# A two-block transformer forward on one core: weight splits placed directly behind the end of a unit, own-engine waits only where a result is used, and the feed-forward loops written out

## The chip, the core and the metric

The kernel runs on one core of a Trainium2 chip. That core has a matrix engine (PE, TensorE), a vector engine (DVE), a scalar engine (ACT), a general engine (POOL) and a sync engine (SP) that here issues only DMAs. Each engine runs its own instructions in order; they meet only at semaphores. The metric is the device time of one execution in microseconds, lower is better.

## The reference

The input is one sequence of 512 tokens with 1024 channels, f32. Block 1 has two layers, block 2 has two layers, and a norm ends each block. The parts with most of the arithmetic are dense products with weights:

```
# block 1, twice
h = h + 0.5 * swiglu_ffn(rms_norm(h, ffn1_norm), w_gate_up, w_down)     # 1024 -> 2*2816 -> 1024
q, k, v, ca, cg = split(rms_norm(h, mix_norm) @ w_in)                   # 14 chunks of 128
mixed = concat([rms_norm(window_attention(q, k, v)), rms_norm(conv31(ca * sigmoid(cg)))])
h = h + mixed @ w_out
h = h + 0.5 * swiglu_ffn(rms_norm(h, ffn2_norm), w_gate_up, w_down)
h = h + sigmoid(h @ w_ple_gate) * rms_norm(p @ w_ple, ple_norm)
# block 2, twice
h = h + concat([gated_deltanet, nsa, stick_breaking]) @ w_out
g, u = split(rms_norm(h) @ w_gate_up)                                   # each through a causal 3-tap conv
h = h + (silu(conv3(g)) * conv3(u)) @ w_down
h = h + sigmoid(rms_norm(h) @ w_ple_gate) * rms_norm(p @ w_ple, ple_norm)
```

## The kernel before

Activations are held transposed: 128 channels on the partitions, 512 tokens along the free axis, eight chunks for the 1024 channels and 22 for the 2816 of the feed-forward. Every dense product is exact to f32 level by splitting both factors into a high and a low half: with activations `xh`, `xl` and weights `wh`, `wl`, PE adds `xh*wh`, `xl*wh` and `xh*wl` (lines L400, L401, L402).

**Units.** The weights stream in 564 units of 128x1024 (512 KB each) through four `raw` buffers. ACT copies a unit to its high half (`act_split`, L380), DVE subtracts that for the low half (`dve_split`, L385), each with two buffers, and PE turns a unit into one 128x512 result in one of two PSUM banks `DB`. A unit of eight chunks has 24 matmuls. The semaphores are `w_hi` and `w_lo` (halves ready), `unit` (PE has finished a unit), `bank` (its result has been read). ACT's split of unit k+2 needs the end of unit k, since it overwrites that unit's `wh`; PE starts unit k+2 when `w_lo` says so and the bank of unit k has been read. The next DMA into a `raw` buffer starts behind the DVE split that reads it.

**Feed-forward.** `ffn_units` cuts the 22 chunks into groups of 8, 8 and 6. Of each group first its gate and up units (two for each chunk), then the eight units of the down-projection, which has as many chunks as the group has. In the first part PE, ACT and DVE each run a hardware loop over pairs of chunks (`Fori`, L509, L522, L543), four units a turn. DVE reads gate (`gbuf`) and up (`ubuf`), multiplies them to `fbuf`, ACT makes `fh`, DVE makes `fl`, and `ff_lo` counts finished chunks. In block 2 each of them first goes through three taps (`act_conv_pair`, `dve_conv_pair`). In the down part DVE adds each result to `h` (L551); in the last group the new `h` chunk is at once split for the next stage (`act_tile` L431 to `xh`, `dve_tile` L467 to `xl`) and squared for its norm (`act_square` L440). All of this, as the split of the weights, stands in one hand-written order for each engine.

**The other dense stages** are straight code: IN (14 units of w_in, whose results are rotated or gated while ACT and POOL run the first 31-tap convolutions), OUT (8 units), GATE (8 units). In each step of them before, the split of unit k+1 comes after all other work of step k-1, and behind nearly every operation of ACT and DVE stands a wait for the engine's own semaphore (as `dve.wait_ge(s["w_lo"], st.up("w_lo"))`). Where a norm's reciprocal is needed (`dve_rstd`, L488; `rstd_e` in OUT of block 1, L1326), DVE makes it ahead of the first result of the stage.

## Time and profile before

| | us |
|---|---|
| median of 3 runs | 4252.59 (4246.54 to 4254.69) |
| profiled execution | 4251.98 |
| its span | 4250.2 |
| PE busy (share of the span) | 3960.5 (93%) |
| DVE busy | 2396.6 (56%) |
| ACT busy | 1667.6 (39%) |
| POOL busy | 471.4 (11%) |
| weight DMAs | 564 of 512 KB, 3.5 median from issue to landing |

The profiled execution has 1.8 us outside its span. A stage lies where its lines are busy: block 1's layer 0 runs FFN1 from 23, IN from 391, OUT from 621, FFN2 from 669 and GATE from 1035; its layer 1 starts at 1092 and its IN at 1454. Block 2's layer 0 has OUT from 2690, its feed-forward groups from 2738, 2860 and 3000 and GATE from 3135; the last GATE is at 4178. In a table of windows a row gives, for each engine, the busy time and in brackets the count of instructions, then PE's granted clock as a share of 2.4 GHz.

### The profile page before, as it was taken

What the parts mean: (1) busy time and instruction counts of PE and PEld (TensorE: products, weight loads), DVE (VectorE), ACT (ScalarE), POOL (GpSimd) and SP (SyncE); (2) the same over time, 40 slices, a digit from 0 to 9 for tenths busy, and PEclk for the clock granted to TensorE, in tenths of its full rate; (3) what the DMA queues carried; (4) which work ended last, traced back from release to release, by engine and by line L of the source; (5) the groups of instructions that cost most, each with busy time, mean ns of one, the idle gap of its engine ahead of it and who ended that gap; (6) DMA issues with size and microseconds to landing.
All of it is one profiled execution on the core that took longest, in us unless ns stands there. A gap on an engine that the chain in (4) does not pass through costs nothing. (4 is left out here: it accounts for less than half of the span.)

```text
span 4250.2 us, 51550 instructions
## 1 busy us (share of the span) xinstructions
PE 3960.5 (93%) x17866; PEld 3110.4 (73%) x17866; DVE 2396.6 (56%) x3149; ACT 1667.6 (39%) x2268; POOL 471.4 (11%) x366
## 2 busy tenths in 40 slices
PE   8999979999999997999989999899989999899997
PEld 6887657888788765788766677677767667777775
DVE  5455765445544576545667634756566663475656
ACT  4224643223322464322434444443343444343333
POOL 1001710000000171000000022100010012110001
PEclk9999989999999998999999989999999989899998
DMA  4333103333333310333321100222223100022221
GB/s 146 95 99 94 55 16 95 99 98 103 89 94 99 94 55 20 97 98 96 105 92 54 35 1 6 70 89 89 91 85 99 50 25 1 11 80 89 89 89 69
DMA packets 86995, 314.55 MB, mean 74 GB/s; under 512 B 10016, under 2 KB 10400, under 8 KB 86176
## 3 DMA queue, kind: packets, MB, share of 16 engines
q1 hardware_dynamic: 83664, 302.43, 22.7%
q10 hardware_dynamic: 3152, 9.74, 0.7%
q8 instruction: 111, 1.82, 0.2%
q14 instruction: 68, 0.56, 0.0%
HBM read 307.94 MB, written 2.10 MB: 73 GB/s over the span
## 5 line engine op out<-in xcount | busy, mean ns | idle before, releaser
L400 PE MATMUL ps<-xh,wh 128*128 128x512 f32 x2336 | 924.2, 396 | 59.3 <-DVE wl L385 40.7
L380 ACT ACTIVATE wh<-raw 128x1024 fp32r<-128x1024 f32 x564 | 598.4, 1061 | 896.2 <-PE ps L402 681.8
L385 DVE TENSOR_TENSOR wl<-raw,wh 128x1024 fp32r<-128x1024 f32 x564 | 712.6, 1263 | 419.5 <-ACT wh L380 399.8
L401 PE MATMUL ps<-xl,wh 128*128 128x512 f32 x2336 | 913.9, 391 | 0.0
L402 PE MATMUL ps<-xh,wl 128*128 128x512 f32 x2336 | 913.5, 391 | 0.0
L400 PEld LDWEIGHTS ps<-xh,wh 128*128 128x128 f32 x2336 | 441.5, 189 | 173.2 <-DVE wl L385 54.0
L400 PE MATMUL ps<-fh,wh 128*128 128x512 f32 x1280 | 511.7, 400 | 49.1 <-DVE fl L1467 28.5
L402 PEld LDWEIGHTS ps<-xh,wl 128*128 128x128 f32 x2336 | 441.2, 189 | 93.1
L401 PEld LDWEIGHTS ps<-xl,wh 128*128 128x128 f32 x2336 | 441.4, 189 | 92.7 <-issue 2.7
L401 PE MATMUL ps<-fl,wh 128*128 128x512 f32 x1280 | 503.6, 393 | 0.0
L402 PE MATMUL ps<-fh,wl 128*128 128x512 f32 x1280 | 502.6, 393 | 0.0
L400 PEld LDWEIGHTS ps<-fh,wh 128*128 128x128 f32 x1280 | 243.1, 190 | 124.0 <-DVE wl L385 38.8
L446 POOL TENSOR_TENSOR rstd<-rstd,sq 128x512 f32<-128x512 f32 x77 | 101.9, 1323 | 1798.3 <-ACT sq L440 1797.5
L402 PEld LDWEIGHTS ps<-fh,wl 128*128 128x128 f32 x1280 | 243.4, 190 | 52.4
L401 PEld LDWEIGHTS ps<-fl,wh 128*128 128x128 f32 x1280 | 243.6, 190 | 49.3 <-issue 0.5
L551 DVE SCALAR_TENSOR_TENSOR h<-ps,h 128x512 f32<-128x512 f32 x144 | 99.6, 692 | 282.7 <-PE ps L402 281.8
L410 PE MATMUL ps<-xh,wh 128*128 128x512 f32 x448 | 198.9, 444 | 25.0 <-PEq L1358 10.0
L733 POOL TENSOR_TENSOR y<-y,tap_out 128x512 f32<-128x512 f32 x120 | 171.9, 1432 | 109.4 <-ACT tap_out L934 101.6
L605 ACT ACTIVATE sbuf<-gbuf 128x512 f32<-128x512 f32 x88 | 55.7, 632 | 326.6 <-DVE gbuf L616 326.6
L412 PE MATMUL ps<-xh,wl 128*128 128x512 f32 x448 | 179.7, 401 | 0.0
L411 PE MATMUL ps<-xl,wh 128*128 128x512 f32 x448 | 179.1, 400 | 0.0
L616 DVE TENSOR_TENSOR gbuf<-ps,rstd 128x512 f32<-128x512 f32 x88 | 60.9, 692 | 155.4 <-PE ps L402 154.6
(464 smaller groups left out, 5270.2 us busy)
## 6 DMA issues: line engine op xcount, KB each, us to landing
raw<-in_w SPq DMA_DIRECT2D x564, 512.0 KB, 3.5
con<-in_consts SPq DMA_DIRECT2D x1, 2052.5 KB, 14.3
h<-in_x SPq DMA_DIRECT2D x4, 512.0 KB, 7.6
p_t<-in_p ACTq DMA_DIRECT2D x4, 512.0 KB, 3.6
w1k<-in_w1c ACTq DMA_DIRECT2D x2, 1024.0 KB, 4.8
w1v<-in_w1c ACTq DMA_DIRECT2D x2, 1024.0 KB, 6.9
out<-h SPq DMA_DIRECT2D x8, 256.0 KB, 2.0
dup_k<-roped ACTq DMA_DIRECT2D x8, 128.0 KB, 2.4
```

The lines of the kernel that those rows point to most:

```text
L380: nc.scalar.activation(wh[k % 2][:, :], raw[k % 4][:, :], ACT.Copy).then_inc(s["w_hi"], 1)
L385: nc.vector.tensor_tensor(wl[k % 2][:, :], raw[k % 4][:, :], wh[k % 2][:, :].bitcast(F32), ALU.subtract).then_inc(s["w_lo"], 1)
L400: nc.tensor.matmul(DB[k % 2][:, :], a, hi(q), start=(q == order[0]), stop=False)
L401: nc.tensor.matmul(DB[k % 2][:, :], a, lo(q), start=False, stop=False)
L402: last = nc.tensor.matmul(DB[k % 2][:, :], b, hi(q), start=False, stop=(q == order[-1]))
L410: nc.tensor.matmul(DB[k % 2][:, :], a, hi(q), start=start and n == 0, stop=False)
L411: nc.tensor.matmul(DB[k % 2][:, :], a, lo(q), start=False, stop=False)
L412: last = nc.tensor.matmul(DB[k % 2][:, :], b, hi(q), start=False, stop=stop and n == len(chunks) - 1)
L446: nc.gpsimd.tensor_tensor(acc[:, :], acc[:, :], sq[:, n % 2, :], ALU.add).then_inc(s["sq_add"], 1)
L551: nc.vector.scalar_tensor_tensor(h[:, j, :], DB[k % 2][:, :], factor, h[:, j, :], ALU.mult, ALU.add).then_inc(s["bank"], 1)
L616: v.tensor_tensor(gbuf[:, :], DB[k % 2][:, :], rstd[:, :], ALU.mult).then_inc(s["bank"], 1)
L733: nc.gpsimd.tensor_tensor(y[:, ct, :], y[:, ct, :], tap_out[:, i % 3, :], ALU.add)\
```

## The change

It has five parts.

- In both splits, the tiles, the squares and the feed-forward bodies the wait for the engine's own semaphore is left out, except where the next operation reads what was just written.
- In the down part of a feed-forward and in IN, OUT and GATE, the split of unit k+2 stands directly behind the read (DVE) or the end (ACT) of unit k, ahead of tile, square, sigmoid, taps and the like. In the swiglu body ACT splits before the silu.
- The loops over pairs of chunks on PE, ACT and DVE are written out: there are six feed-forwards (two in each layer of block 1, one in each of block 2) of three groups, so 18 such stretches, and on each of the three engines none of them is a hardware loop now. PE's program grows from 10536 rows to 14407, DVE's from 2589 to 2947, ACT's from 1767 to 1886.
- `AHEAD = 3`: of the first down unit of a group PE runs all chunks but the last, then three chunks of the second unit, then the last chunk of the first, then the rest of the second.
- In block 2's body the low half `fl` of a chunk is made behind the first read of the next chunk, and ACT starts both first taps before the silu. In the last pair of a group the split of the second down unit comes at the end. In OUT the reciprocals for the embedding's norm move behind the first read.

The diff, cut to its core:

```diff
+AHEAD = 3
...
             nc.scalar.activation(wh[k % 2][:, :], raw[k % 4][:, :], ACT.Copy).then_inc(s["w_hi"], 1)
-            act.wait_ge(s["w_hi"], st.up("w_hi"))
...
                                     ALU.subtract).then_inc(s["w_lo"], 1)
-            dve.wait_ge(s["w_lo"], st.up("w_lo"))
...
-                with pe.Fori(start, n // 2) as i:
+                for i in range(start, n // 2):
                     for k in range(4):
                         pe_unit(pe, s, i, u + k, x_hi, x_lo)
-                for j in range(DC):
-                    k = u + 2 * n + j
-                    wait = (lambda q: ("ff_lo", ff_before + pair + q + 1)) if j == 0 else None
-                    pe_unit(pe, s, 0, k, f_hi, f_lo, n, wait)
-
-        def act_ffn(act, s, st, base, ff_before, gain, x_n, sq_n, pair_body, turns, stat_n, sums=0, dst=xh, trig=False):
+                k = u + 2 * n
+                pe.wait_ge(s["w_lo"], k + 1)
+                pe.wait_ge(s["bank"], k - 1)
+                for q in range(n - 1):
+                    pe.wait_ge(s["ff_lo"], ff_before + pair + q + 1)
+                    pe_chunks(k, f_hi, f_lo, (q,), q == 0, False)
+                pe.wait_ge(s["w_lo"], k + 2)
+                pe.wait_ge(s["bank"], k)
+                pe_chunks(k + 1, f_hi, f_lo, range(AHEAD), True, False)
+                pe.wait_ge(s["ff_lo"], ff_before + pair + n)
+                pe_chunks(k, f_hi, f_lo, (n - 1,), False, True).then_inc(s["unit"], 1)
+                pe_chunks(k + 1, f_hi, f_lo, range(AHEAD, n), False, True).then_inc(s["unit"], 1)
...
                 for j in range(DC):
                     k = u + 2 * n + j
-                    if j > 0:
-                        act_split(act, s, st, 0, k + 1)
+                    if j < DC - 1:
+                        act_split(act, s, st, 0, k + 2)
                     if g == len(GROUPS) - 1:
...
                 for j in range(DC):
                     k = u + 2 * n + j
-                    if j > 0:
-                        dve_split(dve, s, st, 0, k + 1)
                     dve.wait_ge(s["unit"], k + 1)
                     nc.vector.scalar_tensor_tensor(h[:, j, :], DB[k % 2][:, :], factor, h[:, j, :],
                                                    ALU.mult, ALU.add).then_inc(s["bank"], 1)
-                    dve.wait_ge(s["bank"], st.up("bank"))
+                    evicted = st.up("bank")
+                    if j < DC - 1:
+                        dve_split(dve, s, st, 0, k + 2)
                     if g == len(GROUPS) - 1 and gain is not None:
+                        dve.wait_ge(s["bank"], evicted)
                         dve_tile(dve, s, st, j, gain, x_n + j, hi, lo)
...
-                with act.Fori(0, n // 2) as i, st.turns(i, n // 2, turns):
+                for i in range(n // 2):
...
+            act_split(act, s, st, i, k + 2)
             act.wait_ge(s["bank"], i * 4 + (k + 1))
             nc.scalar.activation(sbuf[:, :], gbuf[:, :], ACT.Silu).then_inc(s["silu"], 1)
-            act.wait_ge(s["silu"], st.up("silu"))
-            act_split(act, s, st, i, k + 2)
...
                             for n in range(14):
-                                if n:
-                                    act_split(act, s, st, 0, o + U1_IN + n + 1)
+                                if n < 13:
+                                    act_split(act, s, st, 0, o + U1_IN + n + 2)
...
-                                dve_split(dve, s, st, 0, u + 1)
                                 if n == 0:
+                                    dve_split(dve, s, st, 0, u + 1)
                                     dve_rstd(dve, s, st, 2)
...
                                     .then_inc(s["bank"], 1)
                                 dve.wait_ge(s["bank"], st.up("bank"))
+                                if n < 13:
+                                    dve_split(dve, s, st, 0, u + 2)
...
                                 u = o + U1_OUT + n
-                                if n:
-                                    dve_split(dve, s, st, 0, u + 1)
-                                else:
-                                    dve.wait_ge(s["stat_read"], 3)
-                                    v.reciprocal(rstd_e[:, :], rstd_e[:, :]).then_inc(s["dve_step"], 1)
-                                    dve.wait_ge(s["dve_step"], st.up("dve_step"))
                                 dve.wait_ge(s["unit"], u + 1)
                                 v.tensor_tensor(h[:, n, :], DB[u % 2][:, :], h[:, n, :], ALU.add)\
                                     .then_inc(s["bank"], 1)
                                 dve.wait_ge(s["bank"], st.up("bank"))
+                                if n < DC - 1:
+                                    dve_split(dve, s, st, 0, u + 2)
                                 dve_tile(dve, s, st, n, g("ffn2"), made + 8 + n)
+                                if n == 0:
+                                    dve.wait_ge(s["stat_read"], 3)
+                                    v.reciprocal(rstd_e[:, :], rstd_e[:, :]).then_inc(s["dve_step"], 1)
+                                    dve.wait_ge(s["dve_step"], st.up("dve_step"))
                                 v.scalar_tensor_tensor(e_t[:, n, :], e_t[:, n, :], g("ple")[:, n:n + 1],
                                                        rstd_e[:, :], ALU.mult, ALU.mult).then_inc(s["dve_step"], 1)
...
                     act_split(act, s, st, i, k + 2)
...
+                    first_tap(0)
+                    if chunk + 1 < size:
+                        act_split(act, s, st, i, k + 3)
+                        first_tap(1)
+                        silu()
+                    else:
+                        silu()
+                        first_tap(1)
+                        act_split(act, s, st, i, k + 3)
                     act.wait_ge(s["ff"], n + 1)
...
+                    read(0)
+                    if chunk > 0:
+                        remainder(chunk - 1, n - 1)
                     dve_split(dve, s, st, i, k + 2)
...
+                    later_taps(0)
+                    read(1)
+                    if chunk + 1 < size:
+                        dve_split(dve, s, st, i, k + 3)
+                    later_taps(1)
                     dve.wait_ge(s["silu"], n + 1)
                     v.tensor_tensor(fbuf[:, :], ubuf[:, :], sbuf[:, :], ALU.mult).then_inc(s["ff"], 1)
...
+                    if chunk + 1 == size:
+                        dve_split(dve, s, st, i, k + 3)
+                        remainder(chunk, n)
...
                                 dve.wait_ge(s["bank"], st.up("bank"))
+                                if n < DC - 2 or n == DC - 2 and after:
+                                    dve_split(dve, s, st, 0, u + 2)
                                 dve.wait_ge(s["sig"], n + 1)
```

On ACT, at the start of IN in block 1 (`wh_58`, `wh_59` are the two high buffers, the numbers behind `raw` name the four raw buffers), before:

```order
L959 DMA p_t<-in_p 128x1024
L966 ACT_TABLE_LOAD
L966 ACTIVATE sbuf<-v_t 128x512
L939 ACTIVATE diag<-con,small_73 128x128 x5
L380 ACTIVATE wh_58<-raw_56 128x1024
L939 ACTIVATE diag<-con,small_73 128x128 x6
L380 ACTIVATE wh_59<-raw_57 128x1024
```

and now:

```order
L960 DMA p_t<-in_p 128x1024
L381 ACTIVATE wh_58<-raw_56 128x1024
L967 ACT_TABLE_LOAD
L967 ACTIVATE sbuf<-v_t 128x512
L940 ACTIVATE diag<-con,small_73 128x128 x5
L381 ACTIVATE wh_59<-raw_57 128x1024
L940 ACTIVATE diag<-con,small_73 128x128 x6
L381 ACTIVATE wh_58<-raw_54 128x1024
```

The split into `wh_58` moved from behind the gate's sigmoid (L966 before, L967 now) and the first five diagonal tiles to a place ahead of both, and each later split moved in the same way.

On DVE, in the conv body of block 2, the second half of a turn before (in the loop; ISA and REGISTER_ALU are waits on register values and their arithmetic):

```order
L1452 TENSOR_TENSOR cbuf<-ps,rstd 128x512
...
L385 TENSOR_TENSOR wl_61<-raw_55,wh_59 128x1024
L1456 REGISTER_ALU
...
L1460 SCALAR_TENSOR_TENSOR ubuf<-cbuf,small_74,ubuf 128x512
L1462 REGISTER_ALU
L1464 TENSOR_TENSOR fbuf<-ubuf,sbuf 128x512
L1467 ISA
L1467 TENSOR_TENSOR fl<-fbuf,fh 128x512
```

and now, from the `fl` of the last but one chunk of the first group to the first read of the down part:

```order
L1454 TENSOR_TENSOR fl<-fbuf,fh 128x512
L385 TENSOR_TENSOR wl_60<-raw_56,wh_58 128x1024
L1466 SCALAR_TENSOR_TENSOR ybuf<-cbuf,small_74,ybuf 128x512
L1469 SCALAR_TENSOR_TENSOR ybuf<-cbuf,small_74,ybuf 128x512
L1459 TENSOR_TENSOR cbuf<-ps,rstd 128x512
L1466 SCALAR_TENSOR_TENSOR ubuf<-cbuf,small_74,ubuf 128x512
L1469 SCALAR_TENSOR_TENSOR ubuf<-cbuf,small_74,ubuf 128x512
L1485 TENSOR_TENSOR fbuf<-ubuf,sbuf 128x512
L385 TENSOR_TENSOR wl_61<-raw_57,wh_59 128x1024
L1454 TENSOR_TENSOR fl<-fbuf,fh 128x512
L555 SCALAR_TENSOR_TENSOR h<-ps,h 128x512
L385 TENSOR_TENSOR wl_60<-raw_54,wh_58 128x1024
```

The `fl` of a chunk (L1467 before, L1454 now) moved behind the next read of a gate, and in the last pair of the group the split into `wl_61` moved behind `fbuf` (L1464 before, L1485 now).

On PE, where a group's down part starts (unit k reads `wh_58`, unit k+1 `wh_59`), before:

```order
L400 MATMUL ps<-fh,wh_58 128x512 [waits ff_lo]
L401 MATMUL ps<-fl,wh_58 128x512
L402 MATMUL ps<-fh,wl_60 128x512
L400 MATMUL ps<-fh,wh_58 128x512 [waits ff_lo]
L401 MATMUL ps<-fl,wh_58 128x512
L402 MATMUL ps<-fh,wl_60 128x512
L400 MATMUL ps<-fh,wh_59 128x512 [waits bank,w_lo]
L401 MATMUL ps<-fl,wh_59 128x512
L402 MATMUL ps<-fh,wl_61 128x512
```

and now:

```order
L409 MATMUL ps<-fh,wh_59 128x512 [waits bank,w_lo]
L410 MATMUL ps<-fl,wh_59 128x512
L411 MATMUL ps<-fh,wl_61 128x512
L409 MATMUL ps<-fh,wh_59 128x512
L410 MATMUL ps<-fl,wh_59 128x512
L411 MATMUL ps<-fh,wl_61 128x512
L409 MATMUL ps<-fh,wh_59 128x512
L410 MATMUL ps<-fl,wh_59 128x512
L411 MATMUL ps<-fh,wl_61 128x512
L409 MATMUL ps<-fh,wh_58 128x512 [waits ff_lo]
L410 MATMUL ps<-fl,wh_58 128x512
L411 MATMUL ps<-fh,wl_60 128x512
```

Three chunks of the second unit now stand ahead of the chunk of the first that waits for the last `ff_lo`.

## Rows read from the trace of the kernel before

**Rows 1.** The head of the page.

```profile
span 4250.2 us, 51550 instructions
```

**Rows 2.** PE's waits: released by; us in total, times, longest.

```profile
PE ps L400 <- DVE wl L385: 68.9, 76, 4.1
...
PE ps L400 <- DVE fl L1467: 28.5, 6, 5.7
...
PE ps L410 <- PEq L1358: 10.0, 1, 10.0
```

**Rows 3.** Windows of the dense stages; columns as in the first line.

```profile
core 0: us, PE busy (x) PEld busy (x) DVE busy (x) ACT busy (x) POOL busy (x), PEclk, DMA share, GB/s
34.00:349.00 315.00, 315.00 (x1390) 260.79 (x1391) 150.13 (x177) 92.25 (x105) 0.00 (x0) 1.00 0.33 97
349.00:391.00 42.00, 38.90 (x163) 29.53 (x161) 24.22 (x29) 21.04 (x26) 8.86 (x7) 1.00 0.38 113
391.00:452.00 61.00, 50.87 (x201) 39.83 (x200) 32.31 (x30) 38.27 (x59) 25.11 (x19) 0.92 0.26 78
626.00:669.00 43.00, 40.57 (x175) 31.81 (x173) 32.59 (x31) 19.35 (x24) 9.49 (x7) 1.00 0.28 87
1092.00:1100.00 8.00, 5.84 (x26) 4.50 (x25) 5.31 (x7) 3.38 (x4) 0.00 (x0) 1.00 0.22 66
1454.00:1515.00 61.00, 50.91 (x205) 40.18 (x205) 32.82 (x30) 39.32 (x61) 25.99 (x18) 0.94 0.26 78
2690.00:2738.00 48.00, 46.17 (x196) 36.09 (x196) 37.40 (x33) 20.04 (x25) 9.09 (x7) 1.00 0.27 88
2738.00:2860.00 122.00, 113.21 (x480) 90.83 (x479) 78.19 (x91) 53.88 (x61) 0.00 (x0) 0.97 0.26 86
2925.00:3000.00 75.00, 68.67 (x291) 55.00 (x290) 44.71 (x53) 25.93 (x31) 0.00 (x0) 0.98 0.26 85
3065.00:3133.00 68.00, 58.70 (x242) 45.42 (x241) 41.47 (x49) 30.46 (x39) 7.96 (x7) 0.95 0.28 93
3133.00:3182.00 49.00, 44.17 (x176) 33.56 (x175) 35.31 (x35) 23.99 (x30) 6.97 (x6) 0.97 0.25 82
4178.00:4226.00 48.00, 44.59 (x180) 34.42 (x179) 32.11 (x29) 17.98 (x23) 7.23 (x6) 0.96 0.10 33
```

**Rows 4.** Timeline, down units of the last FFN1 group: start, length, engine, line, names.

```profile
376.78 1.33 DVE L385 TENSOR_TENSOR wl<-raw,wh 128x1024 fp32r<-128x1024 f32 x1 [1.00 <-ACT wh L380]
...
378.17 0.50 PE L400 MATMUL ps<-fh,wh 128*128 128x512 f32 x1 [0.32 <-DVE wl L385]
...
378.94 0.72 ACT L431 ACTIVATE xh<-h,small 128x512 fp32r<-128x512 f32 x1 [2.25 <-DVE h L551]
```

**Rows 5.** Timeline at the start of IN in layer 0 of block 1.

```profile
397.96 0.69 DVE L1161 TENSOR_TENSOR v_t<-ps,rstd 128x512 f32<-128x512 f32 x1
...
402.68 1.23 DVE L385 TENSOR_TENSOR wl<-raw,wh 128x1024 fp32r<-128x1024 f32 x1 [4.02 <-ACT wh L380]
...
403.96 0.79 PE L400 MATMUL ps<-xh,wh 128*128 128x512 f32 x1 [4.06 <-DVE wl L385]
```

**Rows 6.** Timeline at the last conv pair of block 2's last group.

```profile
3093.80 0.63 ACT L1434 ACTIVATE fh<-fbuf 128x512 f32 x1 [3.21 <-DVE fbuf L1464]
...
3095.40 0.79 PE L400 MATMUL ps<-fh,wh 128*128 128x512 f32 x1 [5.68 <-DVE fl L1467]
```

**Rows 7.** Timeline of DVE at the start of OUT in block 1.

```profile
621.50 3.35 DVE L1326 RECIPROCAL rstd_e<-rstd_e 128x512 f32<-128x512 f32 x1
...
626.56 0.69 DVE L1329 TENSOR_TENSOR h<-ps,h 128x512 f32<-128x512 f32 x1 [1.71 <-PE ps L412]
```

**Rows 8.** Groups of POOL by line in 391:486: count, busy, mean ns, idle.

```profile
L733 POOL TENSOR_TENSOR y<-y,tap_out 128x512 f32<-128x512 f32 x34 | 51.1, 1504 | 43.2 <-ACT tap_out L934 41.2
```

**Rows 9.** Groups of DVE by line, whole span: count, busy, mean ns, idle.

```profile
L1460 DVE SCALAR_TENSOR_TENSOR ubuf<-cbuf,small,ubuf 128x512 f32<-128x512 f32 x44 | 33.1, 752 | 6.7 <-DVE ubuf L1457 6.7
...
L1350 DVE TENSOR_TENSOR h<-h,gbuf 128x512 f32<-128x512 f32 x16 | 11.1, 692 | 0.5
```

More of the change, by code:

```diff
@@ L542, in dve_ffn @@
                     dve_rstd(dve, s, st, stat_n)
-                with dve.Fori(0, n // 2) as i, st.turns(i, n // 2, turns):
+                for i in range(n // 2):
                     for k in (0, 2):
-                        pair_body(dve, s, st, i, u + k, i * 2 + k // 2, i * 2 + (ff_before + pair + k // 2), 8 * g)
+                        pair_body(dve, s, st, i, u + k, i * 2 + k // 2, i * 2 + (ff_before + pair + k // 2), 8 * g, n)
                 for j in range(DC):
                     k = u + 2 * n + j
-                    if j > 0:
-                        dve_split(dve, s, st, 0, k + 1)
                     dve.wait_ge(s["unit"], k + 1)
@@ L1352, in _ @@
                                 dve.wait_ge(s["out_done"], st.up("out_done"))
+                                if n < DC - 2 or n == DC - 2 and after:
+                                    dve_split(dve, s, st, 0, u + 2)
                                 if n and after:
@@ new lines, in remainder, with read @@
+                    def remainder(chunk, n):
+                        dve.wait_ge(s["ff_hi"], n + 1)
+                        v.tensor_tensor(fl[:, chunk, :], fbuf[:, :], fh[:, chunk, :].bitcast(F32), ALU.subtract)\
+                            .then_inc(s["ff_lo"], 1)
+                    def read(half):
+                        dve.wait_ge(s["unit"], i * 4 + (k + half + 1))
+                        v.tensor_tensor(cbuf[:, half, 3:], DB[(k + half) % 2][:, :], rstd[:, :], ALU.mult)\
+                            .then_inc(s["bank"], 1)
+                        st.up("bank")
@@ new lines, in later_taps @@
+                    def later_taps(half):
+                        out, sem = ((ybuf, "gate_conv"), (ubuf, "dve_step"))[half]
+                        dve.wait_ge(s["tap0"], n * 2 + 10 + half)
+                        v.scalar_tensor_tensor(out[:, :], cbuf[:, half, 2:2 + T], ftaps[:, w + half, 1:2], out[:, :],
+                                               ALU.mult, ALU.add).then_inc(s["dve_step"], 1)
+                        dve.wait_ge(s["dve_step"], st.up("dve_step"))
+                        v.scalar_tensor_tensor(out[:, :], cbuf[:, half, 1:1 + T], ftaps[:, w + half, 0:1], out[:, :],
+                                               ALU.mult, ALU.add).then_inc(s[sem], 1)
+                        done = st.up(sem)
+                        if half:
+                            dve.wait_ge(s[sem], done)
@@ L2920, in _ @@
                                 dve.wait_ge(s["bank"], st.up("bank"))
+                                if n < DC - 2 or n == DC - 2 and after:
+                                    dve_split(dve, s, st, 0, u + 2)
                                 dve.wait_ge(s["sig"], n + 1)
```

121 lines of the change are left out of this document (42 added, 79 removed).

## The prediction

> **What bounds the kernel now.** I read the page's head first: the span is 4250.2 us [rows 1], and the profiled execution took 4251.98, within 0.02% of the median of 4252.59, so the sum below is made against 4252.0 and stands for the median as well. PE is busy for 93% of it, so the bound is PE, and the only thing this change can move is time in which PE doesn't run at its full rate. Its waits come next: the largest two are for the low half of a unit of weights, 68.9 us in 76 waits, and for the low half of the last feed-forward chunk in block 2, 28.5 us in 6 waits [rows 2]. Both are in places that the change touches.
>
> Waits understate the loss, since PE runs at half clock for some time behind a long one. So I took the loss from windows. In 34:349, the feed-forward loops of block 1, PE does 1390 matmuls in 315.00 us with no idle time: 315.00 / 1390 = 0.2266 us each [rows 3]. A unit of 24 matmuls is 5.44 us, a down unit of the group of six, with 18, is 4.08. What a window is longer than its matmuls times 0.2266 is lost, and that includes the half clock. The reader is to see three things in these rows: the swiglu loops lose nothing, so unrolling and leaner waits have nothing to win there; IN in block 1 loses 61 - 201 x 0.2266 = 15.4 us (its twin, 1454:1515, 14.5) with the clock at 0.92; and every stretch of block 2's feed-forward loses some.
>
> **The change part by part.** For each place: what is lost, what stays, what goes.
>
> Start of a swiglu feed-forward: 1092:1100 loses 8 - 26 x 0.2266 = 2.1 us [rows 3]. It is the largest of eight small places (four starts, two tails of the second feed-forward, two GATEs of block 1); at about 1.1 each they give 9 us. This is an estimate from one row, 0 to 17 us.
>
> Tail of FFN1: 349:391 loses 42 - 163 x 0.2266 = 5.1 us [rows 3]. The timeline shows why: DVE's split starts at 376.78, since ACT made square and tile first, PE starts at 378.17 behind it with 0.32 of idle, and ACT waits 2.25 us for the tile's input while it could split [rows 4]. With the split directly behind the unit's end, the low half is ready 1.06 + 1.33 + some 0.1 = 2.5 us after the unit before last ends, against 4.08 for a unit. The cycle no longer touches PE. Two pieces stay: some 0.4 for the matmuls on the norm's sums, and a new one. With AHEAD the first down unit ends with only three chunks of the second left, 9 x 0.2266 = 2.04 us in the group of six, and the split for the third needs 2.5: 0.4 us. (In the groups of eight five chunks are left, 3.4 us, and it is hidden.) So 5.1 - 0.8 = 4.3 us, twice: 8.6.
>
> IN of block 1: the result of the first unit is read at 397.96, but DVE's next split starts at 402.68, behind ACT's sigmoid and diagonal tiles, and PE resumes at 403.96 after 4.06 us, at half clock [rows 5]. Moved, ACT splits at once at the end of unit n, while DVE reads; DVE's half is ready at 397.96 + 0.69 + 1.23 + 0.1 = 400.0, where the unit beside it runs to about 399.9. What is now late is the sigmoid and the taps, by 1.06 us on ACT and 1.23 on DVE in each step. Behind them wait POOL's additions, 1.504 us each, 34 of them in this stage [rows 8]; at three to a unit they take 4.5 of its 5.44 us, so they still fit. I keep 0.5 a layer: gain 14.9 + 14.0 = 28.9.
>
> OUT of block 1: 626:669 loses 43 - 175 x 0.2266 = 3.3 us [rows 3]. The split is hidden now, but the moved reciprocal isn't free. Before, its 3.35 us ran from 621.50 and ended ahead of the first result, which DVE read at 626.56 after a wait of 1.71 [rows 7]. Behind the first read it stands ahead of the second one: read and split to 629.0, tile to 629.8, reciprocal to 633.1, embedding to 633.9, read to 634.7, split to 636.0, where PE is done with the unit before at 634.6. So 1.4 us are late, and the gain is 3.3 - 1.6 = 1.7, twice: 3.4.
>
> OUT of block 2: 2690:2738 loses 48 - 196 x 0.2266 = 3.6 [rows 3], and 0.9 stays by the same reciprocal, which there starts from an earlier split. Gain 2.7, twice: 5.4.
>
> Block 2's first group: 2738:2860 loses 122 - 480 x 0.2266 = 13.2 us, about half of it in the loop and half at the start of the down part [rows 3]. In the loop the splits came late, behind waits on register values: L1460 waits 6.7 / 44 = 0.15 us behind the operation ahead of it, where straight code with a wait on its own engine (L1350) shows 0.5 / 16 = 0.03 [rows 9]. A pair now takes DVE read, remainder, split, two taps, read, split, two taps and product, 4 x 0.69 + 4 x 0.75 + 2 x 1.23 = 8.2 us with 0.3 for waits, of 10.88 for two units: it fits. At the down part PE waited for the last `fl`, L1467, made behind L1464 and ACT's `fh`. Now PE has seven chunks, 4.76 us, before it needs the second unit's `wl`, which comes 5.2 us after the last up unit (read 0.72, tap on ACT 0.8, two taps 1.6, product 0.75, split 1.25), and the last `fl`, at 5.9, is needed only three chunks on. So 0.5 stays, and 0.2 in the loop. Gain 12.5, twice: 25.
>
> Second group, 2925:3000: 75 - 291 x 0.2266 = 9.1 lost, by the same reasoning 0.9 stays: 8.2, twice 16.4 [rows 3].
>
> Third group and tail, 3065:3133: 68 - 242 x 0.2266 = 13.2 us lost [rows 3]; the wait at 3095.40 alone is 5.68, and half clock follows [rows 6]. In a group of six only five chunks, 3.4 us, cover the 5.2: 1.8 us stay, with 0.6 of the tail as in block 1. Gain 10.8, twice: 21.6.
>
> GATE of block 2: 3133:3182 loses 49 - 176 x 0.2266 = 9.1, the last one (4178:4226) 48 - 180 x 0.2266 = 7.2 [rows 3]. The first split behind the reciprocal came last behind sigmoid and both operations on `h`. Now it is directly behind the read. I keep 1.0 and 1.2: gain 8.1 + 6.0 = 14.1.
>
> Own waits by themselves: L1350's 0.03 us [rows 9] is all that one costs in straight code, and DVE and ACT are off the path there: 0. The bounds are 0 and 0.15 us for each conv pair's step. The Trainium skill, "VectorE: DVE Perf Modes", section "The DRAIN you can't avoid", states that eight copies took 13.88 us with a semaphore after each or only behind the last; by it this part is worth nothing, and the trace agrees with 0.03 us.
>
> Sum: 9 + 8.6 + 28.9 + 3.4 + 5.4 + 25 + 16.4 + 21.6 + 14.1 = 132.4 us. 4252.0 - 132.4 = 4119.6; I say **4120**. SP gains no wait: a weight's DMA starts behind the split that frees its buffer, and splits only come earlier.
>
> **The rivals.**
>
> *The gaps close only in part.* ACT, DVE and POOL now start work in the same moment (split against tap, split against read), and what the stage has beside the weights is moved behind the split. If that sets the pace where DVE's other work is dense, in IN, in block 2's GATE and in the third groups (28.9 + 14.1 + 21.6 + 8.6 = 73 us of the sum), and half of it stays, the time is 4120 + 37 = 4157. For it: DVE is busy 32.31 of 61 us in IN, POOL 25.11, and both wait for ACT. Against it: three additions of POOL leave 0.9 us of room in a unit.
>
> *Everything closes.* The pieces that I keep (0.5 x 2, 1.6 x 2, 0.9 x 2, 0.8 x 2, 0.7 x 2, 0.9 x 2, 2.4 x 2, 2.2) come to 18: 4102. For it: the timelines of before leave slack in most units. Against it: the 5.2 us chain behind the last up unit has no work to cover it in the group of six.
>
> *Slower: the written-out program stalls in its own supply.* PE's program grows by 3871 rows. Once in the trace PE waits 10.0 us for its sequencer [rows 2], at a block's start. If each of the 18 stretches that were loops had one such stall, that is 180 us: 4252 - 132 + 180 = 4300. It decides from 132 / 18 = 7.4 us a stretch. Against it: IN, OUT, the mixing parts and all down parts are straight code already, and 34:349, which has two straight down parts, loses nothing [rows 3]. The Trainium skill, "Runtime: NRT & Kernel Launch", section "Instruction fetch mechanics", says that instructions are refilled ahead in order with the cost of a crossing mostly hidden, and that a taken branch out of the window stalls: it speaks for written-out loops, and no row here has such a stall at a loop.
>
> *No effect.* If PE's wait for `wl` were in truth one for the weight's transfer, the order of the splits would change nothing: 4252. Against it: before the late split at 402.68 the releaser is ACT's `wh`, which is itself behind other work in program order [rows 5].
>
> **How the numbers follow.** Forecast 0.73 (its own range 4108 to 4136), partly closed 0.12, all closed 0.08, slower 0.04, no effect 0.03. A measurement of this kernel tells 0.2%, about 8.5 us, from no change, as the runs before spread by 8. Faster: the first three, 0.93; same 0.03; slower 0.04. To leave out no more than two in ten, with both neighbours inside: 4096 to 4160.
>
> **What would show it.** In the changed profile PE's wait for `wl` should fall from 68.9 to under 20 us, that for the last `fl` from 28.5 to under 5; the window of IN should have a clock of 1.00 and lose under 2 us; in the group of six PE should wait some 1.8 us for the `wl` of the second down unit; in OUT of block 1 one wait of about 1.4 us should stand behind the reciprocal. Waits of PE for its sequencer in the former loops would make the third rival right; a wait for POOL or for `upad` in IN the first. If a window of the swiglu loops loses time where it lost none, I am wrong about what was free there.

## The result, and the profile after

The changed kernel took 4095.31 us (median of 4 runs, 4090.53 to 4100.18), the kernel before, in the same runs, 4249.57 (4243.09 to 4254.69). The ratio is 0.9638, 95% interval 0.9619 to 0.9657: 154 us less. The forecast was 132 less and a range that ended at 4096, so the direction was right and the range too narrow, by 0.7 us. The profiled execution took 4096.91.

The head of the page, the busy row of PE and its clock in 40 slices:

```profile
span 4095.1 us, 47766 instructions
...
PE 3912.0 (96%) x17866; PEld 3105.5 (76%) x17866; DVE 2340.5 (57%) x3149; ACT 1583.4 (39%) x2242; POOL 491.2 (12%) x366
...
PEclk9999979999999997999999989899999998999999
```

The span is 155.1 us shorter than that of [rows 1]. ACT has 26 instructions fewer than before (2242, against 2268), for the same work; that is a first hint at something that the forecast lacked. PE's waits for the low halves of weights, in the changed kernel (released by; total, times, longest):

```profile
PE ps L409 <- DVE wl L385: 6.3, 10, 1.6
...
PE ps L399 <- DVE wl L385: 4.4, 8, 0.9
```

They answer to the 68.9 us of [rows 2], which are nearly gone. The 28.5 us of waits for the last `fl` have no row any more. Windows of the changed kernel's swiglu loops, the FFN1 tail, IN of block 1, and block 2's first group (columns as in [rows 3]):

```profile
34.00:345.00 311.00, 311.00 (x1374) 257.61 (x1373) 144.17 (x176) 85.86 (x101) 0.00 (x0) 1.00 0.33 97
345.00:386.00 41.00, 40.41 (x177) 32.59 (x175) 24.08 (x30) 20.53 (x27) 11.79 (x7) 1.00 0.39 116
386.00:446.00 60.00, 60.00 (x265) 49.19 (x264) 43.24 (x45) 44.67 (x70) 33.92 (x24) 1.00 0.35 106
...
2675.00:2805.00 130.00, 129.56 (x569) 106.34 (x568) 82.86 (x98) 46.63 (x58) 1.34 (x1) 1.00 0.29 97
```

The rate is the old one, 311 / 1374 = 0.2263 us. IN does 265 matmuls in 60 us without idle time and at full clock, where it did 201 in 61 [rows 3].

**Where the time came from.** Both traces hold 17866 matmuls, in the same order except for a few at the down parts. So the time from the n-th to the m-th matmul can be compared directly, stage by stage; the table gives how much shorter it got, both layers together, in us. For dense stages it repeats to 0.1 us between kernels that don't differ there; for the mixing stages only to some 5.

| stage | forecast | measured |
|---|---|---|
| eight small places of block 1 | 9.0 | 9.1 |
| tail of FFN1 | 8.6 | 9.1 |
| IN of block 1 | 28.9 | 31.7 |
| OUT of block 1 | 3.4 | 4.6 |
| OUT of block 2 | 5.4 | 6.1 |
| block 2, first groups | 25.0 | 25.6 |
| block 2, second groups | 16.4 | 18.5 |
| block 2, third groups and tail | 21.6 | 22.2 |
| GATE of block 2 | 14.1 | 13.7 |
| sum of these | 132.4 | 140.6 |
| IN of block 2 | 0 | 13.6 |
| mixing, block 1 and block 2 | 0 | -3.9 and +3.0 |

Not all of it is time without work: PE's busy time fell by 48.5 us (3960.5 to 3912.0) for the same matmuls. The granted clock stood at the lower of its two levels, 1.2 GHz, for 336 us before and for 283 us now.

The terms of the sum came out well. What was missing is a stage that the sum didn't have: IN of block 2, whose order wasn't changed. All that changed in it is that the two weight splits no longer wait for their own semaphore, and for that the forecast had 0.

### The profile page after: what moved, and what is told of

Read it like the earlier page. It is cut to its first block and busy times, and to the rows that moved or that the text cites. A ratio compares the mean times of both kernels' runs of the same rounds, so it can differ in the third digit from the quotient of the medians.

```text
span 4095.1 us, 47766 instructions
## 1 busy us (share of the span) xinstructions
PE 3912.0 (96%) x17866; PEld 3105.5 (76%) x17866; DVE 2340.5 (57%) x3149; ACT 1583.4 (39%) x2242; POOL 491.2 (12%) x366
## 5 line engine op out<-in xcount | busy, mean ns | idle before, releaser
L385 DVE TENSOR_TENSOR wl<-raw,wh 128x1024 fp32r<-128x1024 f32 x564 | 693.8, 1230 | 201.8 <-ACT wh L381 197.8
L399 PE MATMUL ps<-fh,wh 128*128 128x512 f32 x1016 | 397.3, 391 | 4.4 <-DVE wl L385 4.4
L400 PE MATMUL ps<-fl,wh 128*128 128x512 f32 x1016 | 395.4, 389 | 0.0
L401 PE MATMUL ps<-fh,wl 128*128 128x512 f32 x1016 | 395.3, 389 | 0.0
L443 POOL TENSOR_TENSOR rstd<-rstd,sq 128x512 f32<-128x512 f32 x77 | 116.4, 1512 | 1693.7 <-ACT sq L438 1692.7
L399 PEld LDWEIGHTS ps<-fh,wh 128*128 128x128 f32 x1016 | 190.7, 188 | 48.2 <-DVE wl L385 8.3
L401 PEld LDWEIGHTS ps<-fh,wl 128*128 128x128 f32 x1016 | 190.7, 188 | 39.8
L400 PEld LDWEIGHTS ps<-fl,wh 128*128 128x128 f32 x1016 | 190.7, 188 | 39.6 <-issue 0.5
L625 DVE TENSOR_TENSOR ubuf<-ps,rstd 128x512 f32<-128x512 f32 x88 | 60.9, 692 | 264.7 <-PE ps L401 264.7
## 6 DMA issues: line engine op xcount, KB each, us to landing
con<-in_consts SPq DMA_DIRECT2D x1, 2052.5 KB, 14.1
```

The lines of the kernel that those rows point to most:

```text
L385: nc.vector.tensor_tensor(wl[k % 2][:, :], raw[k % 4][:, :], wh[k % 2][:, :].bitcast(F32), ALU.subtract).then_inc(s["w_lo"], 1)
L399: nc.tensor.matmul(DB[k % 2][:, :], a, hi(q), start=(q == order[0]), stop=False)
L400: nc.tensor.matmul(DB[k % 2][:, :], a, lo(q), start=False, stop=False)
L401: last = nc.tensor.matmul(DB[k % 2][:, :], b, hi(q), start=False, stop=(q == order[-1]))
L443: nc.gpsimd.tensor_tensor(acc[:, :], acc[:, :], sq[:, n % 2, :], ALU.add).then_inc(s["sq_add"], 1)
```

## The experiments

Times are medians; where there is a ratio to the kernel before, its 95% interval stands behind it. The table above, for each of these kernels, gives the place.

**The splits' own waits, alone and put back.** The edit on the kernel before:

```diff
             nc.scalar.activation(wh[k % 2][:, :], raw[k % 4][:, :], ACT.Copy).then_inc(s["w_hi"], 1)
-            act.wait_ge(s["w_hi"], st.up("w_hi"))
...
                                     ALU.subtract).then_inc(s["w_lo"], 1)
-            dve.wait_ge(s["w_lo"], st.up("w_lo"))
```

> The kernel before with one edit: the waits of the two weight splits for their own semaphores are left out, all else as before. Theory A (an own wait costs about 0.12 us, since without it the next operation starts 0.08 to 0.09 us ahead of the end of the one before instead of 0.03 us behind it, and in block 2's IN, where DVE's chain paces PE, this adds up and takes half-clock stretches away): block 2's IN gets 5 to 7 us shorter in each layer, the rest of the kernel 5 to 15 us in all; time 4249.6 - 25 = 4225. Rival B (own waits are worth nothing, and block 2's IN got shorter by what stands ahead of it): 4250, and block 2's IN within 1 us of before.

Measured: 4175.69 us, 0.9825 (0.9804 to 0.9845), 71 us from these two lines. Block 2's IN got 5.0 and 6.3 us shorter, as theory A said; the six groups of block 2 got 38 us shorter, GATE of block 2 5.5. (In the groups the splits' waits were still waits on register values in a loop, see below.) Rival B is out, and my 25 us were far too few. Then the same lines put back in the changed kernel:

> The changed kernel with one edit: the two weight splits wait for their own semaphores again. Theory A: block 2's IN loses its 13.6 us of gain again (5 to 7 in each layer), and elsewhere, where splits are off PE's path now, 2 to 6 us: 4095.3 + 17 = 4112. Rival B: 4095, block 2's IN as in the changed kernel.

Measured: 4111.37, 0.9677 (0.9658 to 0.9697), 16 us over the changed kernel. Of the 13.6 us in block 2's IN 11.4 go again, and in the six groups nothing. So once loops are written out and splits stand early, these waits matter only where ACT and DVE still set the pace.

**Why a wait costs that.** Two mechanisms show. The small one is in DVE's timeline of the changed kernel, where the split has no wait behind it:

```profile
2997.42 1.22 DVE L385 TENSOR_TENSOR wl<-raw,wh 128x1024 fp32r<-128x1024 f32 x1
2998.55 0.75 DVE L1466 SCALAR_TENSOR_TENSOR ybuf<-cbuf,small,ybuf 128x512 f32<-128x512 f32 x1
2999.34 0.75 DVE L1469 SCALAR_TENSOR_TENSOR ybuf<-cbuf,small,ybuf 128x512 f32<-128x512 f32 x1
```

The tap starts at 2998.55, 0.09 us before the split ends at 2998.64. Where a wait is kept (between the two taps) the next starts 0.04 behind the end. Over all splits of the two kernels the medians are 0.083 us ahead of the end without a wait and 0.035 us behind it with one. So an own wait is worth about 0.12 us, not the 0.03 that the idle column shows. ACT does the same with 0.095 us of overlap. The large one is ACT's function table. In the kernel before, at a place of block 2's IN:

```profile
2174.20 1.06 ACT L380 ACTIVATE wh<-raw 128x1024 fp32r<-128x1024 f32 x1 [6.15 <-PE ps L412]
2184.58 1.28 ACT L1539 ACT_TABLE_LOAD   x1 [9.32 <-DVE rows_k L1579]
2185.87 0.22 ACT L1539 ACTIVATE tiny<-rows_k 128x24 f32<-128x24 f32 x1
```

In the changed kernel, at the same place:

```profile
2121.62 1.06 ACT L381 ACTIVATE wh<-raw 128x1024 fp32r<-128x1024 f32 x1 [5.59 <-PE ps L411]
2122.70 1.28 ACT L1556 ACT_TABLE_LOAD   x1
2131.59 0.22 ACT L1556 ACTIVATE tiny<-rows_k 128x24 f32<-128x24 f32 x1 [7.62 <-DVE rows_k L1596]
```

Before, the 1.28 us load ran behind the wait of 9.32 us for DVE and so on the path; now it runs in ACT's idle time, and only the operation itself waits. The order of instructions with their waits says why:

```
before:  L1539 ACT_TABLE_LOAD [waits tok_ready]
         L1539 ACTIVATE tiny<-rows_k 128x24 [waits w_hi]
now:     L1556 ACT_TABLE_LOAD
         L1556 ACTIVATE tiny<-rows_k 128x24 [waits tok_ready]
```

With two waits ahead of an operation, the own one and a foreign one, the foreign one lands on the load that is put in front. Of the 127 table loads of the kernel before 57 started more than 0.2 us behind the operation ahead of them; in the changed kernel 15 of 101, with the waits put back 40 of 101.

**The two engines apart.** The own wait put back on ACT alone, then on DVE alone, in the changed kernel.

> The changed kernel with the own wait behind the weight split put back on ACT alone. Theory L (an own wait on ACT ahead of another wait takes the next operation's place at that wait, so that a function table's load, 1.28 us, runs behind the wait instead of ahead of it): the load counts behind a wait rise from 15 to about 40, block 2's IN loses 4.5 to 6 of its 7 us in each layer, and the time is near that with both put back, 4108. Theory A (each own wait costs 0.12 us on either engine, and those on DVE decide): 4100, and IN loses under 2 us a layer.

Measured: 4106.40, 0.9667 (0.9651 to 0.9683). 40 loads stand behind a wait again, and IN of block 2 loses 3.6 and 5.1 us.

> The changed kernel with the own wait behind the weight split put back on DVE alone. Theory L: DVE has no tables, so block 2's IN loses under 1.5 us a layer, 4097. Theory A: IN loses 4 us or more a layer, 4105 or more.

Measured: 4101.53, 0.9654 (0.9638 to 0.9671); IN loses 2.7 and 1.9 us, with 15 loads behind a wait. So theory L explains the larger part (8.8 of the 11.4 us on its own), but its bound of 1.5 for DVE is passed: the 0.12 us are real as well. They are not additive (8.8 + 4.6 is over 11.4), and part of it is the clock. Windows over the same 1280 matmuls of that stage, before, and with both waits put back, and changed:

```profile
2146.60:2429.20 282.60, 273.23 (x1281) 197.43 (x1280) 198.05 (x348) 118.12 (x188) 9.96 (x7) 0.98 0.19 64
```

```profile
2096.60:2378.20 281.60, 273.02 (x1281) 197.22 (x1280) 198.09 (x348) 118.12 (x188) 9.98 (x7) 0.98 0.20 64
```

```profile
2095.60:2371.30 275.70, 269.81 (x1282) 195.35 (x1281) 196.71 (x348) 115.64 (x187) 9.95 (x7) 0.99 0.20 66
```

Of the 5.9 us between the last two, 3.2 are in PE's busy time: the same matmuls, with 6.7 us of that stretch at 1.2 GHz instead of 13.3.

**One more own wait.** Behind DVE's read in block 2's IN, in the changed kernel:

```diff
-                                    dve.wait_ge(s["bank"], st.up("bank"))
+                                return st.up("bank")
...
                                 dve_split(dve, s, st, 0, o + n + 1)
+                                if n:
+                                    dve.wait_ge(s["bank"], read)
```

> The changed kernel with one more own wait out of the way: in block 2's IN DVE waits for its own read of a result only behind the split that follows it, not ahead of it. Theory A (0.12 us for each own wait, on the path there): some 27 reads a layer, of which about 20 are followed by the split at once, 0.12 x 20 = 2.4 us at most, 1 to 3 us in each layer with the clock's share; 4092. Rival B: no change.

Measured: 4092.71 in one run; IN 0.7 us longer in one layer and 1.0 shorter in the other. No gain that can be told, where theory A had 1 to 3 a layer. The traces show that its count was too high: only 14 of the 27 splits of the first layer stand directly behind such a read, five of these wait for ACT's half anyway, and nine now start early instead of 0.03 us behind. That is 9 x 0.12 = 1.1 us at most. Behind the splits themselves 19 of 27 operations start early in the changed kernel, 2.3 us at most, against the 2.7 and 1.9 us that the wait cost on DVE alone. The sizes fit; that even the 1.1 us didn't come stays open.

**Loops written out.**

```diff
-                with pe.Fori(start, n // 2) as i:
+                for i in range(start, n // 2):
...
-                with act.Fori(0, n // 2) as i, st.turns(i, n // 2, turns):
+                for i in range(n // 2):
```

(and the same on DVE), in the kernel before:

> The kernel before with only the loops over pairs of chunks written out (waits, order and all else as before). Theory A: own waits on register values cost 0.15 us instead of 0.03 in a loop, so block 2's conv loops, which lose time, gain: 3 to 5 us in each first group, 2 to 3 in the others, some 15 us in all, 4235; block 1's loops gain nothing. Rival B (loops cost nothing that PE sees): 4250. Rival C (the longer program stalls PE): over 4260, with waits of PE for its sequencer in the former loops.

Measured: 4212.35, 0.9911 (0.9890 to 0.9931), 35 us from this alone: 48 us in block 2's groups, some given back elsewhere (6 of it at the starts of block 1's feed-forwards, see below). It has no new wait of PE for its sequencer, so rival C, and with it the slower rival of the prediction, is out. The traces offered two causes: ACT's table loads in the loops (33 at L605, L380 and L1426, and 7 once written out), and DVE's register waits. So each engine's loop was written out alone:

> The kernel before with only ACT's loops over pairs written out; PE and DVE keep theirs. The written-out kernel of the earlier run gained 48 us in the six conv groups of block 2. Theory T (the loop's turns cost ACT two loads of its function table, 1.28 us each, in each turn of two pairs; written out there are none): 35 us or more of the 48 come. Theory R (the waits on register values, 0.15 to 0.26 us each, on DVE are what costs): 15 us or less come.

> The kernel before with only DVE's loops over pairs written out; PE and ACT keep theirs. Theory T: ACT's table loads stay, so 15 us or less of the 48 come in the conv groups. Theory R: 30 us or more.

Measured, one run each: ACT alone 4249.69, with 4.9 us gained in the six groups; DVE alone 4214.77, with 41.3 of the 48. Theory T falls, theory R holds; for PE's loop, which was not written out by itself, 2 us are left. That ACT's edit moves the whole time by nothing is a sum of two things: what the groups gain is lost again at the four starts of block 1's feed-forwards, 1.2 us at three of them and some 3 at the fourth. Before, the load for the silu ran ahead of the loop, in idle time:

```profile
26.52 1.28 ACT L605 ACT_TABLE_LOAD   x1 [0.18 <-ACT rstd L482]
30.74 0.63 ACT L605 ACTIVATE sbuf<-gbuf 128x512 f32<-128x512 f32 x1 [2.94 <-DVE gbuf L616]
```

With ACT's loops written out the load stands behind the wait for `gbuf`, on the path:

```profile
30.41 1.28 ACT L605 ACT_TABLE_LOAD   x1 [4.45 <-DVE gbuf L616]
31.71 0.63 ACT L605 ACTIVATE sbuf<-gbuf 128x512 f32<-128x512 f32 x1
```

Groups of DVE's taps in the kernel before:

```profile
L1445 DVE SCALAR_TENSOR_TENSOR ybuf<-cbuf,small,ybuf 128x512 f32<-128x512 f32 x44 | 33.1, 752 | 13.9 <-DVE wl L385 13.9
L1457 DVE SCALAR_TENSOR_TENSOR ubuf<-cbuf,small,ubuf 128x512 f32<-128x512 f32 x44 | 33.1, 752 | 11.4 <-DVE wl L385 11.4
```

and with DVE's loops written out:

```profile
L1457 DVE SCALAR_TENSOR_TENSOR ubuf<-cbuf,small,ubuf 128x512 f32<-128x512 f32 x44 | 33.1, 752 | 1.6
...
L1445 DVE SCALAR_TENSOR_TENSOR ybuf<-cbuf,small,ybuf 128x512 f32<-128x512 f32 x44 | 33.1, 752 | 1.6
```

Behind a wait on a register value DVE idles 13.9 / 44 = 0.32 and 11.4 / 44 = 0.26 us, where straight code has 0.04. The loop's end costs more, as DVE's timeline of before shows:

```profile
2765.38 0.69 DVE L1467 TENSOR_TENSOR fl<-fbuf,fh 128x512 f32 x1 [1.04 <-ACT fh L1434]
2766.50 0.69 DVE L1441 TENSOR_TENSOR cbuf<-ps,rstd 128x512 f32<-128x512 f32 x1 [0.43 <-DVE fl L1467]
```

Inside a turn the same read starts 0.04 us behind `fl`. From the first read of a pair (L1441) to that of the next DVE takes 11.5 to 12.2 us before, and, but for the first pair of a group, 10.8 to 11.4 with the splits' waits off in the loops and 10.5 to 10.9 (once 11.2) with all loops written out. PE needs 10.88. So the loop's waits and turns are what kept a DVE pair over PE's time. How much of it the waits are and how much the turn, no run separates.

**The place of the splits.** Put back late in IN of block 1, the down parts and block 2's GATE, in the changed kernel (shown for IN; the others alike):

```diff
-                                if n < 13:
-                                    act_split(act, s, st, 0, o + U1_IN + n + 2)
+                                if n:
+                                    act_split(act, s, st, 0, o + U1_IN + n + 1)
```

> The changed kernel with the splits of IN in block 1, of all down parts and of GATE in block 2 put back to where they stood (split of k+1 at the start of a step, behind all other work of the last one); waits, written-out loops, AHEAD and the conv body as changed. Theory A (the place of the split is what closed these gaps): IN of block 1 loses 31.7 - 3.9 us again, the tails of FFN1 9, those of the second feed-forward 1, the tails in block 2 some 6, GATE of block 2 13.7: 57 us, 4152. Rival (the leaner waits closed them): under 15 us, 4110.

Measured: 4139.70, 0.9734 (0.9715 to 0.9754), 44 us over the changed kernel by the medians, 41 by the two ratios. IN loses 27.6 of 31.7, the tails of FFN1 8.1 of 9.1, the third groups 8.8, GATE of block 2 6.9 of 13.7. With 2.4 in the tails of the second feed-forward that is 54 us; some 9 come back, most of it in the mixing stages. The place is the cause in IN and the tails. In GATE half of the gain stays without it; the kernel before with only its splits' waits off gained 5.5 there, so the leaner waits can explain most of that half. In IN the same kernel gained only 4.1 and 0.2. OUT was not put back in either block, so what closed its 10.7 us is not shown.

**AHEAD.** PE's plain order at the down parts, in the changed kernel:

```diff
-                for q in range(n - 1):
-                    pe.wait_ge(s["ff_lo"], ff_before + pair + q + 1)
-                    pe_chunks(k, f_hi, f_lo, (q,), q == 0, False)
...
+                for j in range(DC):
+                    k = u + 2 * n + j
+                    wait = (lambda q: ("ff_lo", ff_before + pair + q + 1)) if j == 0 else None
+                    pe_unit(pe, s, 0, k, f_hi, f_lo, n, wait)
```

> The changed kernel with PE's old order at the start of a down part: the first unit whole, then the second. The last fl is then needed after five or seven chunks instead of three chunks later. In block 2 it comes 5.5 us after the last up unit's end; with five chunks (3.4 us) that is 2.1 us of wait in the third groups against 1.4 now, in the first and second groups 0.8 against 0.2. In block 1, where fl is ready earlier, nothing, and the 0.4 us wait for the third unit goes. With the clock's share: 3 to 8 us longer, 4101. Rival (AHEAD is what closed the 28.5 us of waits for fl): 20 us or more longer, 4118.

Measured: 4094.09, 0.9633 (0.9613 to 0.9652): no difference. AHEAD gives block 2's groups 3.8 us and takes 0.6 in each of block 1's four tails, 2.4; together too small to be told. Without AHEAD 7.6 us of waits for `fl` come back; of the 28.5 [rows 2] the loops written out alone had left 12.5. So most of them were not closed by it.

**The conv body.** The old body, own waits and all, in the changed kernel's written-out code (the whole of `act_conv_pair` and `dve_conv_pair` as before, so no diff is shown).

> The changed kernel with block 2's conv body in its old order and with its old own waits (in written-out code, splits without own waits). Theory A (the order of the body closes the gap at the down parts, and the rest of the groups' gain is from leaner code): of the 66 us gained in the six groups, 4 us each at the six down parts and 1 us a group in the loop come back: 30 us, 4125. Rival (waits and written-out code alone gave the groups' gain): under 8 us, 4102. Rival (all of it is the order): 60 us, 4155.

Measured: 4091.28, 0.9624 (0.9606 to 0.9642). Nothing is lost; the six groups gained 69.8 us in all, against 66.3 with the new body. The first rival was right, beyond its number: the new order of the body gives nothing. It even takes 3.5 us, about what the late split in its last pair costs (4.0, below).

**The two moves that the forecast called costly.** In OUT of block 1 the reciprocal stands behind the first read; DVE in the changed kernel:

```profile
606.15 0.69 DVE L1327 TENSOR_TENSOR h<-ps,h 128x512 f32<-128x512 f32 x1 [5.13 <-PE ps L411]
...
609.13 3.34 DVE L1335 RECIPROCAL rstd_e<-rstd_e 128x512 f32<-128x512 f32 x1
...
613.30 0.69 DVE L1327 TENSOR_TENSOR h<-ps,h 128x512 f32<-128x512 f32 x1
614.02 1.23 DVE L385 TENSOR_TENSOR wl<-raw,wh 128x1024 fp32r<-128x1024 f32 x1
```

and PE there, which waits 0.92 us for that split:

```profile
615.30 0.50 PE L399 MATMUL ps<-fh,wh 128*128 128x512 f32 x1 [0.92 <-DVE wl L385]
```

DVE now idles 5.13 us ahead of the first read, where the reciprocal had its place before [rows 7]. Put ahead of it again:

```diff
                                 u = o + U1_OUT + n
+                                if n == 0:
+                                    dve.wait_ge(s["stat_read"], 3)
+                                    v.reciprocal(rstd_e[:, :], rstd_e[:, :]).then_inc(s["dve_step"], 1)
+                                    dve.wait_ge(s["dve_step"], st.up("dve_step"))
```

> The changed kernel with the reciprocal in OUT of block 1 ahead of the first read again; the splits stay early. It then runs before PE has the first result (before, DVE waited 1.71 us behind it), so nothing is late: OUT of block 1 gets 1 to 1.4 us shorter in each layer, 2 to 3 us in all, 4093. Rival (the first read gets late by it, since other work now ends later): no change or 1 us longer.

Measured: 4089.72 in one run; OUT 1.26 and 1.24 us shorter. Right in place and size. In the last pair of block 2's third group, changed kernel:

```profile
3004.71 0.69 DVE L1485 TENSOR_TENSOR fbuf<-ubuf,sbuf 128x512 f32<-128x512 f32 x1
3005.32 1.22 DVE L385 TENSOR_TENSOR wl<-raw,wh 128x1024 fp32r<-128x1024 f32 x1
...
3006.59 0.50 PE L409 MATMUL ps<-fh,wh 128*128 128x512 f32 x1 [1.58 <-DVE wl L385]
...
3012.07 0.50 PE L399 MATMUL ps<-fh,wh 128*128 128x512 f32 x1 [0.43 <-DVE wl L385]
```

PE waits 1.58 us for the low half behind `fbuf`, and then 0.43 for that of the third down unit. With that split directly behind the read, as in the other pairs:

```diff
                     read(1)
-                    if chunk + 1 < size:
-                        dve_split(dve, s, st, i, k + 3)
+                    dve_split(dve, s, st, i, k + 3)
                     later_taps(1)
```

> The changed kernel with the last conv pair of a group as all others: ACT and DVE split the second down unit directly behind the read, ahead of taps and product. The low half for it is then there before PE has done the first down unit's five chunks, but the last fl comes some 1.2 us later, 6.8 us after the last up unit instead of 5.5; PE needs it after 8 chunks, 5.4 us, in a group of six and after 10, 6.8 us, in a group of eight. So the third groups wait some 0.9 to 1.4 us (1.36 now) and the others 0 to 0.2: from 2 us shorter to no change, 4094. Rival (fl is what decides, and it is later): 3 us longer.

Measured: 4091.55 in one run; the third groups 1.0 us shorter each, the other four 0.5 each, 4.0 in all. That is above the 2 of the expectation, since the other groups gain too.

**All together.**

> The changed kernel with four edits together: the reciprocal in OUT of block 1 ahead of the first read (2.5 us, by the earlier run), the last conv pair of a group as all others (4.0 in the six groups), PE's plain order at the down parts of block 1 (2.4: 0.6 in each of four tails) and the own wait behind the read in block 2's IN put behind the split (2 to 6). If they add up: 4095.3 - 12 = 4083, 0.3% under the changed kernel. If one takes another's gain, 4088.

Measured: 4087.11 (5 runs), 0.9617 (0.9603 to 0.9631). The medians stand 8 us under the changed kernel, the intervals overlap, so it is not shown to be faster. In the traces the parts show: OUT 2.6, the groups 4.0, the tails of block 1 2.3 us; block 2's IN got 1.7 us shorter in its first layer and 0.3 longer in its second, against 2 to 6 in the expectation.

## Why the prediction was right and where it was wrong

**The method held.** Loss as the length of a window less its matmuls at 0.2266 us, minus what a new timeline leaves, gave nine terms that are within 3 us each and 8.2 us in all. Most of that 8.2 is in IN of block 1 (2.8) and in the second groups (2.1). In IN I kept 0.5 a layer and nothing stayed; the rest of the 2.8 lies behind 452, where my window ended [rows 3] and PE waited once more before (0.73 us at 466.19). That the eight small places came out at 9.1 against 9 is luck: they were one row times eight, with bounds of 0 and 17. The pieces said to stay did: 1.58 us in the third group (1.8 forecast), 0.43 us for the third down unit (0.4), 0.92 behind the reciprocal (1.4).

**The step that failed is "own waits by themselves: 0".** L1350's idle time of 0.03 us [rows 9] was read as the price of a wait. It is the distance with one; the distance without is negative, -0.08 us in the median, and no row of before showed it beside that line. And on ACT the larger price is not a distance at all but the place of a 1.28 us table load. Block 2's IN holds six such loads in a layer behind waits (the first at 2152.94), none of which I looked at, because the diff has no line in that stage; the splits that it calls are the change. That left 13.6 us out, and with the 8.2 and the mixing stages' -0.9 it makes 153.3 instead of 132.4. The Trainium skill, "ScalarE: Activation LUTs", section "What ACT_TABLE_LOAD costs", gives both prices on ACT, about 1283 ns for a load and about 93 ns of overlap between operations back to back; the 1.28 and 0.095 us here agree, and neither stood in my sum. It also gives about 1380 ns of draining to each switch, which these rows don't show: the load at 2122.70 starts 0.02 us behind the operation ahead of it, and the operation at 2185.87 0.01 us behind the load. The Trainium skill, "VectorE: DVE Perf Modes", section "The DRAIN you can't avoid", says that for eight copies a semaphore after each costs nothing extra, and I leaned on it. The same section says that a next operation that isn't held starts earlier, which I passed over. Here the trace decides: without the wait these operations start 0.08 us early, as in that second sentence, and the wait put back on DVE alone takes 4.6 us in that stage.

**Right in sum, wrong in reason.** For block 2's groups I named AHEAD, the new order of the body and the later `fl` as what closes the gaps. The runs say otherwise: written-out loops alone give 48 of the 66 us, and the old body with its own waits, in written-out code with only the splits' waits off, gives 70. Of the 18 us behind the 48 the place of the splits in the third groups' tails is worth 8.8 and AHEAD 3.8; the order of the body is worth nothing. My step "the splits came late, behind waits on register values" named the right cause, at 0.15 us; with 0.32 and 0.26 behind the splits and 0.43 at the loop's end it fits the down parts too: the last chunk would be late by what the loop had piled up, and the loops written out alone took the waits for `fl` from 28.5 to 12.5 us.

**The rivals.** "Everything closes" (4102) was nearest, for another reason: the pieces stayed. "Gaps close in part" has no support in IN, where PE doesn't idle in 60 us. "Slower" is out, as there is no stall in the written-out code, and "no effect" by the waits for `wl`, 68.9 us before, of which 10.7 are left. The range ended where my kept pieces ended; it held nothing for a term that I had put to 0 with a bound of 0.15 us on block 2's conv body alone.

## What to carry to other kernels

Take a helper that is called everywhere as a change to every stage, and ask of each stage that has waits in it what the helper's last instruction does there. A wait for an engine's own semaphore cost more here than the idle time behind it shows: compare it with a place that has none, and on ACT look whether a table load stands ahead of a foreign wait or behind it. In a hardware loop on an engine that is close to the pace of the busiest one, count the idle time behind every wait on a register value and at the turn before blaming the order of the body.

## What the runs showed that I had not expected

- On ACT a second wait ahead of an operation that needs another table moved the 1.28 us load behind the foreign wait: 57 of 127 loads before, 15 of 101 after, 40 of 101 with one line put back. Part of the fall from 57 is the loops: with them alone written out it is 43 of 101.
- ACT's loops held 26 table loads of 1.28 us that written-out code doesn't need; taking them away moved the time by nothing (4249.69). It gave 4.9 us in block 2's groups and took 6 at four starts in block 1, where the load that had run ahead of the loop now stood behind a wait.
- At a loop's turn DVE idled 0.43 us, behind a wait on a register value 0.15 to 0.32, where straight code has 0.04; a plain own wait cost 0.12.
- Two lines in two helpers, the splits' own waits, made 71 of the 154 us when they were the only edit, and 16 when everything else had been done: gains that share a gap don't add.
